# Which engine leads the meeting between stages: TensorE instead of GpSimd

## What is computed

```
def first_block(x, ...):
    for l in range(DEPTH):
        h = rms_norm(x, attn_norm[l])
        proj = h @ w_in[l]
        ...
        mix = jnp.concatenate([ret_o, nsa_o, gm_o], axis=-1)
        x = x + (mix @ w_out[l])
        h = rms_norm(x, ffn_norm[l])
        gate, up = jnp.split(h @ w_gate_up[l], 2, axis=-1)
        x = x + ((jax.nn.silu(gate) * up) @ w_down[l])
    return x
```

## Time and profile before

| | |
|---|---|
| median of 3 runs | 3680.62 us (3680.31 to 3689.42) |
| the profiled execution | 3679.47 us, of which the span from first to last instruction is 3677.7 us |
| PE busy | 3532.1 us (96%) |
| DVE busy | 2072.4 us (56%) |
| ACT busy | 861.0 us (23%) |
| POOL busy | 354.0 us (10%) |
| granted TensorE clock, mean | 0.986 |

### The profile page before, as it was taken

One profiled execution on the slowest core, in us unless ns is written; L12 is line 12 of the kernel. 1 busy time (PEld: TensorE's weight loads), 2 busy tenths in 40 slices (PEclk: granted clock), 3 DMA queues, 4 the chain that ended last, 5 costly groups with the idle time before them and its releaser, 6 DMA issues.

```text
span 3677.7 us, 59267 instructions
## 1 busy us (share of the span) xinstructions
PE 3532.1 (96%) x25468; PEld 2914.8 (79%) x25468; DVE 2072.4 (56%) x2865; ACT 861.0 (23%) x1640; POOL 354.0 (10%) x320
## 2 busy tenths in 40 slices
PE   8999999999999999989998999999999999989998
PEld 6777888877778887879897987788888787668886
DVE  3654777636547776645555555632235653864347
ACT  2233101212330012443343331100011212720011
POOL 0000000000000000015403520120000001502000
PEclk9999999999999999999999999999999999999999
DMA  4311444323014443210010031111111231012222
GB/s 168 107 36 50 177 183 173 142 97 98 24 67 183 183 160 122 100 36 3 20 47 25 3 122 58 58 69 58 69 58 69 93 132 46 1 69 93 102 92 92
DMA packets 51316, 320.57 MB, mean 87 GB/s; under 512 B 6988, under 2 KB 7500, under 8 KB 16504
## 3 DMA queue, kind: packets, MB, share of 16 engines
q1 hardware_dynamic: 30240, 220.21, 16.3%
q10 hardware_dynamic: 20824, 96.65, 7.5%
HBM read 299.94 MB, written 9.56 MB: 84 GB/s over the span
## 4 chain that ended last, share of the span: by engine, by line
PE 78%; DVE 7%; PEld 6%; DMA 3%; issue 2%; ACT 2%; PEldq 1%; POOLq 0%; ACTq 0%; POOL 0%; DVEq 0%; SPq 0%; another core or an unknown queue 0%
PE psum L532 19%; PE psum L533 19%; PE psum L534 19%; PE psum L2480 4%; PE psum L2487 4%; DMA pieces_in<-pieces 2%; PEld psum L532 2%; PEld psum L534 2%; PEld psum L533 2%; PE psum L1320 1%; PE psum L1293 1%; PE psum L1304 1%; PEldq L473 1%; PE psum L2617 1%; PE psum L3430 1%
## 5 line engine op out<-in xcount | busy, mean ns | idle before, releaser
L532 PE MATMUL psum<-xt_operands,pieces_hi 128*128 128x512 f32 (+1 forms) x2544 | 940.2, 370 | 23.5 <-DVE xt_operands L783 10.1
L533 PE MATMUL psum<-xt_operands,pieces_hi 128*128 128x512 f32 (+1 forms) x2544 | 928.3, 365 | 0.0
L534 PE MATMUL psum<-xt_operands,pieces_lo 128*128 128x512 f32 (+1 forms) x2544 | 927.8, 365 | 0.0
L532 PEld LDWEIGHTS psum<-xt_operands,pieces_hi 128*128 128x128 f32 x2544 | 481.2, 189 | 109.6 <-issue 20.0
L532 PE MATMUL psum<-pieces_hi,xt_operands 128*128 128x512 f32 x1338 | 531.6, 397 | 15.2 <-DVE pieces_lo L579 11.2
L534 PEld LDWEIGHTS psum<-xt_operands,pieces_lo 128*128 128x128 f32 x2544 | 481.0, 189 | 77.0
L533 PEld LDWEIGHTS psum<-xt_operands,pieces_hi 128*128 128x128 f32 x2544 | 481.6, 189 | 73.0
L533 PE MATMUL psum<-pieces_lo,xt_operands 128*128 128x512 f32 x1338 | 524.1, 392 | 0.0
L534 PE MATMUL psum<-pieces_hi,xt_operands 128*128 128x512 f32 x1338 | 524.0, 392 | 0.0
L589 DVE TENSOR_TENSOR pieces_lo<-pieces_in,pieces_hi 128x2048 fp32r<-128x2048 f32 x190 | 443.6, 2335 | 5.3
L546 DVE CAST pieces_hi<-pieces_in 128x2048 fp32r<-128x2048 f32 x190 | 237.7, 1251 | 307.3 <-PE psum L532 146.4
(11 more groups left out here) (374 smaller groups left out, 4217.4 us busy)
## 6 DMA issues: line engine op xcount, KB each, us to landing
pieces_in<-pieces SPq DMA_DIRECT2D x210, 1024.0 KB, 4.9
x_mem<-ada ACTq DMA_DIRECT2D x28, 1024.0 KB, 4.9
arena<-ada ACTq DMA_DIRECT2D x20, 1024.0 KB, 4.9
arena<-mods ACTq DMA_DIRECT2D x8, 512.0 KB, 15.1
arena<-arena ACTq DMA_DIRECT2D x32, 128.0 KB, 4.3
xt_values<-arena ACTq DMA_DIRECT2D x8, 384.0 KB, 7.6
x_park<-x_mem ACTq DMA_DIRECT2D x1, 3072.0 KB, 14.1
o_park<-arena ACTq DMA_DIRECT2D x2, 1536.0 KB, 5.1
```

What stands on the lines that cost most here:

```text
L532: signal_later(k, pe.matmul(out, sh, mh, start=start, stop=False))
L533: signal_later(k, pe.matmul(out, sh, ml, start=False, stop=False))
L534: return pe.matmul(out, sl, mh, start=False, stop=stop)
```

## The change

`stage_end` now serves ScalarE, VectorE and GpSimd. TensorE runs the new `stage_end_pe`. It empties `k.later`, drains, waits for three arrivals, clears the 128 semaphores and releases VectorE, ScalarE and GpSimd, in this order. Three engines arrive and three are released, as before; GpSimd has a go semaphore now, and TensorE no longer uses its own.

```
-        self.go = {"pe": sem("go_pe"), "act": sem("go_act"), "dve": sem("go_dve")}
+        self.go = {"pe": sem("go_pe"), "act": sem("go_act"), "dve": sem("go_dve"), "pool": sem("go_pool")}
...
-                    stage_end(k, e, "pe")
+                    stage_end_pe(k, e)
...
-                    stage_end_pool(k, e)
+                    stage_end(k, e, "pool")
...
 def stage_end(k, e, name):
 
-    while name == "pe" and k.later:
-        signal_later(k, e.eng.drain())
     e.eng.drain().then_inc(k.S.arrived, 1)
     e.eng.wait_ge(k.S.go[name], 1)
     e.eng.sem_clear(k.S.go[name])
     e.n = 0
 
 
-def stage_end_pool(k, e):
-
+def stage_end_pe(k, e):
+
+    while k.later:
+        signal_later(k, e.eng.drain())
     e.eng.drain()
     e.eng.wait_ge(k.S.arrived, 3)
     e.eng.sem_clear(k.S.stage_range)
-    for name in ("pe", "act", "dve"):
+    for name in ("dve", "act", "pool"):
         e.eng.sem_inc(k.S.go[name], 1)
     e.n = 0
```

## The result

The changed kernel took 3695.43 us (median of 7 runs, 3692.4 to 3702.05), the kernel before 3683.05 in its 7 (3680.31 to 3689.42). The ratio is 1.0035, with a 95% interval of 1.0023 to 1.0047. The median lies just above the range of the forecast, on the slower side. A second comparison, with 11 and 27 runs, gave less: 3695.53 against 3689.4, a ratio of 1.0017 (1.0008 to 1.0026). The intervals overlap only just. The changed kernel takes the same time in both; it is the kernel before that differs by 6 us. Much of what follows is about why.

What follows compares the result with a forecast made beforehand. The prediction took TensorE's chain as the bound, with every engine waiting for the clear at 23 meetings. Its terms, -0.96 + 0.84 + 0.16 + 0.16 - 0.3 + 0.5 = +0.4 us, on 3680.62 gave 3681.0 us, range 3668 to 3695.

Steps and rivals of the forecast that it cites:

- Term 6: At the 23 meetings, the clear of 128 semaphores takes 0.74 us on TensorE against GpSimd's 0.718: +0.5 us.
- rival C: TensorE clears slowly: 1.34 us, 0.62 more at every meeting, 3694.8 us in its first price; chance 0.16.
- Its own sign of being wrong: TensorE's clear under 0.24 or over 1.2 us, or its first work moved over 0.5 us for another reason.
- Equal sequencer rates: By the skill's equal rates alone, TensorE's clear would also take 0.718 us and the clear's term would be 0.
- Terms 2, 3 and 4: Behind the clear: TensorE's start 0.12 us later (+0.84), ScalarE's release 0.02 later (+0.16), GpSimd's memset 0.08 later (+0.16).
- Term 1: VectorE's release rides on the clear, 0.16 us earlier at the 6 meetings where it leads on: -0.96 us.
- Term 5: The late last increment in GpSimd's queue at meeting 6 goes with GpSimd's role as leader: -0.3 us.
- within 0.3%: Forecast that the changed kernel's time cannot be told from the kernel before, 11.0 us either way; chance 0.71.
- Rival D: Changed idleness behind meetings makes TensorE's lower-clock stretches, 1.7 us each, come or go: 3671 to 3691 us; chance 0.09.

Runs made afterwards that it cites:

- the first experiment: The kernel before, GpSimd still leading, with one more clear of 40 semaphores ahead of its clear of 128 at each meeting; 3691.99 us against 3687.93, ratio 1.0011.

## Why the prediction was wrong

*Term 6, the clear of 128 on TensorE, is the step that failed.* The prediction put it at 0.74 us, "TensorE's surplus at about 0.02 us, paid once in a clear". It is 0.989 us. The surplus is paid for every semaphore: 7.5 ns against GpSimd's 5.3. That is 23 x 0.27 = 6.2 us instead of 0.5. The mechanism of rival C was the right one, at about two fifths of its first price: 0.27 us more where it had 0.62. The clue was in the earlier trace rows, where TensorE's single clear is the longest. The prediction used it and then took the difference for a fixed one. Its own sign of being wrong, under 0.24 or over 1.2 us, was set too wide to catch this: 0.989 lies between.

*Equal sequencer rates.* The Trainium skill (Advanced Engine Details and Errata, Clock Domains) gives the sequencers of ScalarE, GpSimd and TensorE the same rate. The clear takes 615, 718 and 989 ns on them, so that rate alone does not carry the sum, as the prediction said.

*Terms 2, 3 and 4, the releases behind the clear, were right in kind and too small.* Gaps between TensorE's instructions are 0.10 to 0.13 us, where the prediction had taken GpSimd's 0.06. TensorE's own start moves by 0.46 to 0.48 at the meetings shown, by some 0.2 apart from the clear (forecast 0.12). ScalarE's moves by 0.36, by 0.09 apart from the clear (forecast 0.02), GpSimd's memset by 0.48, by 0.21 apart from it (forecast 0.08).

*Term 1 held.* Apart from the longer clear VectorE is released 0.18 us earlier (0.99 - 0.90 - 0.27), forecast 0.16. With the longer clear it is 0.09 later, so the one gain of the change is more than eaten up.

*Term 5 held.* Meetings 0 and 6 now show nearly the same idleness, where they had 3.24 and 3.58:

```profile
113.86 0.50 PE L532 MATMUL psum<-pieces_hi,xt_operands 128*128 128x512 f32 x1 [3.36 <-DVE pieces_lo L579]
...
841.54 0.50 PE L532 MATMUL psum<-pieces_hi,xt_operands 128*128 128x512 f32 x1 [3.35 <-DVE pieces_lo L579]
```

It was no accident of one execution: the second profile of before shows 3.24 and 3.58 again, and GpSimd's last increment stands 0.41 us behind the one before it at meeting 6, 0.06 elsewhere. With one more clear in its queue (the first experiment) the delay has moved, to the gap between the two clears at meeting 5 (0.37 us, 0.03 elsewhere), and meeting 6 shows the same idleness as meeting 0:

```profile
749.39 0.20 POOLq L484
749.60 0.37 issue
749.97 0.72 POOLq L485
```

```profile
114.24 0.50 PE L534 MATMUL psum<-pieces_hi,xt_operands 128*128 128x512 f32 x1 [3.51 <-DVE pieces_lo L581]
...
842.06 0.50 PE L534 MATMUL psum<-pieces_hi,xt_operands 128*128 128x512 f32 x1 [3.51 <-DVE pieces_lo L581]
```

So it comes once in each of the six profiles with GpSimd in the lead, at a place that depends on what stands in its queue, and the change did away with it. Its cause stays open.

*The sum, with what was measured:* 7 x 0.48 for TensorE, 7 x 0.36 for ScalarE, 2 x 0.48 for GpSimd, 6 x 0.09 for VectorE, less 0.3, makes 7.1 us. (The prediction counted 8 meetings for ScalarE; the chain shows 7. Behind the last of the 23, at 3675.2, no work follows.) The MLP stage's 0.32 us, times 22, makes 7.0. That is 0.19%. The second comparison found 6.1 us (3 to 10), and 5.4 at equal clock, which agrees; the first found 12.4 (8.5 to 17), which is more. The ratio of the first, 1.0035, is above "within 0.3%", though its interval reaches below it; the sum and the second comparison are within. The sign was not foreseen: the sum should have read +7, and the forecast 3688.

*Rival D, the clock, was real and drawn too narrow on one side.* The forecast was set on the median of three runs, 3680.62, as if it were the kernel's own. Two of the three were near the lower edge of what this kernel does, which was bad luck: the range ended 0.4 us below the measured median. With +7.1 on the 3683.05 of its 7 runs one comes to 3690.2, and the changed kernel's 7 runs came out 5 us above that. Most of these 5 us lie with before, not with the change: the changed kernel's median is the same in both comparisons, 3695.43 and 3695.53, and before's is 3683.05 in the one and 3689.4 in the other. Whether the 7 first runs were a lucky draw or had another cause is open, as said above. The tie that D drew between idleness and the lower level does not hold run by run: behind the same 3.58 us of idleness at meeting 6, the second profile of before starts on the upper level, its first matmul taking 0.50 us and not 0.80 as in the earlier trace rows. In sum a longer meeting can bring more of the lower level, as the clear done twice shows with 0.75 us; at the 0.3 us of this change it is a us or two at most.

## What to carry to other kernels

A meeting of all engines is a path in which the leader's semaphore instructions count, so read what each of them costs on the engine that is to lead, and let one lead that is quick at it. Whatever the leader does behind the clear also delays its own next work; that cost TensorE 0.29 us. Clear only what the stage has used: that gave 11 us, and GpSimd instead of TensorE in the lead 5 to 6. And before a difference of 0.3% is explained, take a second profile of the kernel before, which here moved by nearly half of what there was to explain, and compare runs of equal granted clock.

## What the hardware showed that was not expected

- One instruction that clears 128 semaphores takes 0.615 us on ScalarE, 0.718 on GpSimd, 0.802 on VectorE and 0.989 on TensorE. Its time grows with the number: 5.3 ns for each on GpSimd, 7.5 on TensorE, and on ScalarE 4.3 ((343 - 76) / 62), each between 9 and 71 semaphores.
- TensorE's semaphore instructions follow each other with gaps of 0.10 to 0.13 us behind the clear at the meetings shown, GpSimd's increments with 0.06 to 0.07. Two clears in a row on GpSimd have only 0.03 between them.
- The same stage of the same kernel, 460 matmuls with the same work around them, took 45.15 us at a mean granted clock of 0.92 in one execution and 48.19 at 0.86 in another.
- Late in that stage, in the first profile of before, TensorE had been busy for 3.90 of 5.40 us when the clock fell from its upper level, 2.4 GHz, to the lower, 1.2 GHz (PEclk 1.00, then 0.50). How long it then stays there differs from one execution to the next: 6.7 us here (the first fence), twice that in the changed kernel (221.2 to 234.8, the second).

```profile
216.00:221.40 5.40, 3.90 (x35) 3.79 (x35) 1.28 (x2) 0.60 (x1) 0.00 (x0) 1.00 0.01 3
221.50:228.20 6.70, 6.70 (x24) 5.15 (x24) 1.62 (x4) 0.82 (x2) 0.00 (x0) 0.50 0.00 0
```

```profile
221.20:234.80 13.60, 13.60 (x47) 10.50 (x48) 3.99 (x8) 0.82 (x2) 0.00 (x0) 0.50 0.14 46
```
